# A sixteenth of a PEER layer's experts computed densely beside the gathers of the others

## The reference

```python
q = (ht @ wq).reshape(T, 8, 2, 128)                          # T = 256 tokens, 8 heads
sc = einsum('thpd,hpnd->thpn', q, subkeys)                   # 2 x 128 key scores a head
v1, i1 = top_k(sc[:, :, 0], 16);  v2, i2 = top_k(sc[:, :, 1], 16)
cand = v1[..., :, None] + v2[..., None, :]                   # 256 sums
best, pos = top_k(cand, 16)
experts = i1[pos // 16] * 128 + i2[pos % 16]                 # 16 of 16384 experts, a head
gates = softmax(best)
act = gelu(einsum('tkd,td->tk', u_tab[experts], xb))         # u_tab, v_tab: 16384 x 1024
out = einsum('tk,tkd->td', gates * act, v_tab[experts])
```

## Time and profile before

| | us |
|---|---|
| median of 3 runs | 1186.43 (1185.9 to 1187.0) |
| the profiled execution | 1191.29 |
| its span, first to last instruction | 1189.3 |
| mean granted TensorE clock over the span | 0.988 |

### The profile page before, as it was taken

One profiled execution on the slowest core, in us unless ns is written; L12 is line 12 of the kernel. 1 busy time (PEld: TensorE's weight loads), 2 busy tenths in 40 slices (PEclk: granted clock), 3 DMA queues, 4 the chain that ended last, 5 costly groups with the idle time before them and its releaser, 6 DMA issues.

```text
span 1189.3 us, 14690 instructions
## 1 busy us (share of the span) xinstructions
PE 1055.9 (89%) x4770; PEld 714.6 (60%) x4770; DVE 674.6 (57%) x1469; ACT 531.0 (45%) x1302; POOL 688.3 (58%) x431
## 2 busy tenths in 40 slices
PE   9998998888898877877777778999999999999998
PEld 6874554445454322322232224998999997888886
DVE  2577888877576576784774447323455553521323
ACT  5866434433422322323223235546666435544544
POOL 5734444344444434443344333985797986988885
PEclk9999999999999999899999999999999999999999
DMA  7779999999999999999999997763445554655552
GB/s 254 266 271 422 405 422 420 421 421 422 421 420 421 423 420 420 390 422 422 421 422 422 418 420 296 240 231 111 160 159 160 183 179 153 211 180 195 192 182 102
DMA packets 66530, 372.26 MB, mean 313 GB/s; under 512 B 7672, under 2 KB 8800, under 8 KB 33632
## 3 DMA queue, kind: packets, MB, share of 16 engines
q0 software_dynamic: 37152, 268.45, 54.5%
q1 hardware_dynamic: 26800, 97.02, 24.3%
q10 hardware_dynamic: 2512, 5.94, 1.5%
HBM read 369.80 MB, written 1.06 MB: 312 GB/s over the span
## 4 chain that ended last, share of the span: by engine, by line
PE 53%; DMA 30%; DVE 6%; ACT 5%; issue 4%; POOL 2%; DVEq 0%; ACTq 0%; SPq 0%; POOLq 0%
DMA arena<-in_peer_uv,idx_all 29%; PE ps L1993 12%; PE ps L1680 10%; PE ps L1682 10%; PE ps L1681 10%; PE ps L1704 5%; PE ps L1705 3%; DVE arena L1450 2%; DVE arena L1581 1%; PE ps L2053 1%; ACT prob L807 1%; DMA arena<-in_peer_v,idx_all 1%; POOL w_hl L478 1%; ACT wts L801 1%; POOL arena L494 1%
## 5 line engine op out<-in xcount | busy, mean ns | idle before, releaser
L1993 PE MATMUL ps<-arena,prob 128*128 128x512 f32 x1024 | 476.0, 611 | 117.9 <-ACT prob L807 111.1
L494 POOL DMA_INDIRECT arena<-in_peer_uv,idx_all x254 | 276.0, 1086 | 375.6 <-PE ps L1993 334.2
L478 POOL TENSOR_TENSOR w_hl<-ring,w_hl 128x1024 fp32r<-128x1024 f32 x146 | 368.2, 2534 | 103.5 <-ACT w_hl L585 102.7
L1993 PEld LDWEIGHTS ps<-arena,prob 128*128 128x128 f32 x1024 | 188.3, 193 | 389.8 <-issue 198.9
L1450 DVE CUSTOM_DVE_ANT_0 arena<-arena,xn 128x1024 f32<-128x1024 f32 x256 | 312.2, 1224 | 188.1 <-DMA arena<-in_peer_uv,idx_all 184.8
L794 ACT ACTIVATE gel<-acts 128x2 f32<-128x2 f32 (+1 forms) x131 | 26.7, 204 | 401.2 <-DVE acts L1450 400.8
L585 ACT ACTIVATE w_hl<-ring 128x1024 fp32r<-128x1024 f32 x157 | 165.6, 1060 | 84.1 <-PE ps L1682 80.9
L1680 PE MATMUL ps<-xT,w_hl 128*128 128x256 f32 x568 | 164.1, 289 | 2.4 <-POOL w_hl L478 1.8
L1682 PE MATMUL ps<-xT,w_hl 128*128 128x256 f32 x568 | 161.4, 284 | 0.0
L1681 PE MATMUL ps<-xT,w_hl 128*128 128x256 f32 x568 | 161.3, 284 | 0.0
L1680 PEld LDWEIGHTS ps<-xT,w_hl 128*128 128x128 f32 x568 | 109.6, 193 | 3.8 <-POOL w_hl L478 2.3
(11 more groups left out here) (324 smaller groups left out, 1322.1 us busy)
## 6 DMA issues: line engine op xcount, KB each, us to landing
ring<-in_weights SPq DMA_DIRECT2D x174, 512.0 KB, 3.2
arena<-in_peer_uv,idx_all POOLq DMA_INDIRECT x254
held<-in_weights SPq DMA_DIRECT2D x4, 512.0 KB, 5.7
arena<-in_rg_weights ACTq DMA_DIRECT2D x1, 2048.0 KB, 8.7
bias<-rel_scratch ACTq DMA_DIRECT2D x1, 1024.0 KB, 8.7
arena<-in_subkeys SPq DMA_DIRECT2D x1, 1024.0 KB, 7.1
out_x<-x ACTq DMA_DIRECT2D x4, 256.0 KB, 2.1
arena<-in_band SPq DMA_DIRECT2D x1, 768.0 KB, 7.3
```

What stands on the lines that cost most here:

```text
L478: pool.tensor_tensor(pair[:, 1], raw(n), pair[:, 0].bitcast(F32), ALU.subtract).then_inc(w_lo, 1)
L494: pool.indirect_dma_start(uv_slot(n), None, A["peer_uv"], bass.IndirectOffsetOnAxis(idx_all[:, h, c:c + 1], 0))\
L1993: j = pe.matmul(banks(2 + 2 * t + half), diag[:, n % GRING, :], uv_slot(n)[:, D + half * 512:D + (half + 1) * 512], start=(h == 0 and c % ...
```

## The change

The last 1024 experts (8 values of the first key, "rows") are computed for all 256 tokens from sixteen more weight tiles: eight of the transposed u rows (DU), eight of the v rows (DV). DU and DV are loaded by SyncE behind the query weights, from about slot 82, and are split in high and low at the slots listed (ScalarE `*_HI`, GpSimd `*_LO`).

- Scores: 8 tiles x 12 products into banks 0, 1, 6, 7 behind slots 122, 128, ... 164. One gelu pass of four parts on ScalarE at slot 176, into `x`.
- Gates by threshold: for each head and tile GpSimd adds the two keys' scores for the 1024 experts (128 x 1024); ScalarE exponentiates them; VectorE keeps those at or above the head's 16th best (`least`), multiplies by the softmax's reciprocal sum and adds them to `dense_gates`. That is 16 sums, 16 exponentials and 32 passes of VectorE, at slots 108 to 190.
- Values: gelu times gate (VectorE, slots 190 and 192), 16 transposes (TensorE, 196 and 198), high and low parts into `xT`, and 8 tiles x 12 products behind slots 204, 208, ... 232, added in the banks of the experts.
- Gathers from slot 8 on get `bounds_check=SPARSE - 1` (15359) with `oob_is_err=False`: a row beyond it isn't fetched and the place keeps what lay there. Its gate is multiplied by zero. The first eight gathers fetch all rows. As a left-over row may be used several times, the dot's product goes to a scratch row from slot 12 on, no longer in place; to slot 66 there is one scratch row, and each dot waits for the one before.
- The top-k of heads 3 to 7 starts at slots 64, 80, 96, 112, 128, the gates 16 slots later, with their own buffers (`late_gates`).

```diff
+DENSE_ROWS = 8
+SPARSE_ROWS = NKEYS - DENSE_ROWS
+SPARSE = SPARSE_ROWS * NKEYS
+ODOT_FROM = 12
+BOTH_FROM = 66
+TOPK_FROM = {3: 64, 4: 80, 5: 96, 6: 112, 7: 128}
+DU_HI, DU_LO, DU_AT = ([a + 6 * c for c in range(8)] for a in (108, 119, 122))
+DENSE_EXPS = {0: 108, 1: 120, 2: 132, 3: 144, 4: 154, 5: 164, 6: 174, 7: 184}
+DENSE_GELU = 176
+DENSE_TURN = 196
+DV_AT = [204 + 4 * r for r in range(8)]
+DV_HI = [154 + 6 * r for r in range(4)] + [206 + 4 * r for r in range(4)]
+DV_LO = [a + 11 for a in DV_HI]
@@ sync
+            for n in range(W_DU, W_X2):
+                next_weight(n)
             sp_.wait_ge(v_apart[APART - 1], 16)
@@ gpsimd
                 pool.indirect_dma_start(uv_slot(n), None, A["peer_uv"],
-                                        bass.IndirectOffsetOnAxis(idx_all[:, h, c:c + 1], 0))\
+                                        bass.IndirectOffsetOnAxis(idx_all[:, h, c:c + 1], 0),
+                                        bounds_check=SPARSE - 1, oob_is_err=False)\
+            def dense_key_sums(j):
+                h, t = divmod(j, NT)
...
+                if j >= 2:
+                    pool.wait_ge(dense_kept, j - 1)
+                lanes = scores_of(h).rearrange("p (r n) -> p r n", r=4)
+                pool.tensor_tensor(key_sums(j), bc(lanes[:, 2 * t + 1, :], 1, DENSE_ROWS),
+                                   bc(lanes[:, 2 * t, SPARSE_ROWS:], 2, NKEYS), ALU.add).then_inc(dense_sum, 1)
+            def dense_turn(n):
+                for h, at in DENSE_EXPS.items():
+                    if n in (at + 6, at + 7):
+                        dense_key_sums(2 * h + n - at - 6)
+                if n in DU_LO:
+                    pool.wait_ge(w_lo, W_DU)
+                    split_lo(W_DU + DU_LO.index(n))
+                if n in DV_LO:
+                    split_lo(W_DV + DV_LO.index(n))
@@ scalar
+            def dense_exps(h):
+                for t in range(NT):
+                    j = 2 * h + t
+                    act.wait_ge(dense_sum, j + 1)
+                    act.wait_ge(tk, topk_at(h, t) + 9)
+                    if j >= 2:
+                        act.wait_ge(dense_added, j - 1)
+                    act.activation(key_exps(j), key_sums(j).rearrange("p r n -> p (r n)"), ACT.Exp,
+                                   bias=nbest[:, h, t:t + 1], scale=rinv[:, t:t + 1]).then_inc(dense_exp, 1)
+            def dense_gelus():
+                act.wait_ge(w_used, W_DU + 8)
+                for t in range(NT):
+                    for half in range(2):
+                        act.activation(x[:, t, HALVES[half]], dense_bank(t, half), ACT.Gelu,
+                                       scale=rinv[:, t:t + 1]).then_inc(dense_gelu, 1)
@@ vector
+            def dense_add(j):
...
+                dve.wait_ge(dense_exp, j + 1)
+                dve.scalar_tensor_tensor(out=kept, in0=key_sums(j).rearrange("p r n -> p (r n)"),
+                                         scalar=least[:, h, t:t + 1], in1=kept,
+                                         op0=ALU.is_ge, op1=ALU.mult).then_inc(dense_kept, 1)
...
+                dve.scalar_tensor_tensor(out=dense_gates[:, t, :], in0=kept, scalar=exr[:, h, t:t + 1],
+                                         in1=dense_gates[:, t, :], op0=ALU.mult, op1=ALU.add).then_inc(dense_added, 1)
+                out = u
+                if n >= ODOT_FROM:
+                    out = row_gain[:] if n < BOTH_FROM or n % 2 == 0 else spare_row
...
+                    elif n > ODOT_FROM:
+                        dve.wait_ge(dots_done, n if n <= BOTH_FROM else n - 1)
-                dve.tensor_tensor_reduce(u, u, xn[:, c // TOPK, :], 1.0, 0.0, ALU.mult, ALU.add,
+                dve.tensor_tensor_reduce(out, u, xn[:, c // TOPK, :], 1.0, 0.0, ALU.mult, ALU.add,
-                if 1 < h < PH - 1 and c < TOPK_STAGES:
-                    topk_stage(h + 1, c)
+                for hh, at in TOPK_FROM.items():
+                    if at <= n < at + TOPK_STAGES:
+                        topk_stage(hh, n - at)
@@ tensor
+            def dense_scores(c):
+                w = weight(W_DU + c)
...
+                for t in range(NT):
+                    for half in range(2):
+                        i = matmul3(dense_bank(t, half).rearrange("p (c n) -> p c n", n=P),
+                                    parts(xT, c, slice(t * P, (t + 1) * P)), parts(w, slice(4 * half, 4 * half + 4)),
+                                    c == 0, c == NC_ - 1)
+                i.then_inc(w_used, 1)
+            def dense_values(r):
+                w = weight(W_DV + r)
+                for t in range(NT):
+                    pe.wait_ge(dense_lo, 2 * t + r // 4 + 1)
+                    for half in range(2):
+                        i = matmul3(banks(2 + 2 * t + half).rearrange("p (c n) -> p c n", n=P),
+                                    parts(xT, r, slice(t * P, (t + 1) * P)), parts(w, slice(4 * half, 4 * half + 4)),
+                                    False, False)
+                i.then_inc(w_used, 1)
```

More of the change, by code:

```diff
@@ L169, in build @@
         w_hl = sb("w_hl", [P, SPLIT, 2, NC_, P], F32R)
+        with nc.sbuf_tensor("dense_gates", [P, NT, 1024], F32) as dense_gates:
+            pass
         extra_hl = sb("extra_hl", [P, 2, NC_, P], F32R)
@@ L396, in scores_of, with gates_of, key_sums, key_exps @@
             return sc_all[:, h, :] if h else sc_head0
+        def gates_of(h):
+            return gates[:, h % 2, :] if h < 4 else late_gates[:, h - 4, :]
+        def key_sums(j):
+            return held[:, j % 2, :].rearrange("p (r n) -> p r n", n=NKEYS)
+        def key_exps(j):
+            return held[:, 2 + j % 2, :]
+        def dense_bank(t, half):
+            return banks(DENSE_BANKS[2 * t + half])
         def turn_cols(n, count):
@@ L426, in next_weight @@
             def next_weight(n):
+                at = turn_of(n) % RING
                 sp_.wait_ge(w_lo, n - RING + 1)
-                sp_.dma_start(ring[:, n % RING, :], A["weights"][n]).then_inc(w_ready[n % RING], 16)
+                sp_.dma_start(ring[:, at, :], A["weights"][n]).then_inc(w_ready[at], 16)
             sp_.dma_start(sinks[:], A["sinks"].broadcast_to([P, HEADS])).then_inc(sinks_ld, 16)
@@ L777, in gate_exps, with dense_highs, dense_turn @@
                 for t in tiles:
[L778 to L779 removed]
+                    act.activation(ex[:, h % 2, t, :], best[:, t, :], ACT.Exp, bias=nbest[:, h, t:t + 1],
+                                   scale=rinv[:, t:t + 1], accum_out=exs[:, h, t:t + 1]).then_inc(ex_done, 1)
+            def dense_exps(h):
[13 more added lines that the diff above has]
+                                       scale=rinv[:, t:t + 1]).then_inc(dense_gelu, 1)
+            def dense_highs(t):
+                for half in range(2):
+                    act.wait_ge(dense_turned, 2 * t + half + 1)
+                    act.activation(xT[:, 0, 4 * half:4 * half + 4, t * P:(t + 1) * P],
+                                   dense_bank(t, half).rearrange("p (c n) -> p c n", n=P),
+                                   ACT.Identity).then_inc(dense_hi, 1)
+            def dense_turn(n):
+                for c in range(8):
+                    if n == DU_HI[c]:
+                        split_hi(W_DU + c)
+                    if n == DV_HI[c]:
+                        split_hi(W_DV + c)
+                for h, at in DENSE_EXPS.items():
+                    if n == at:
+                        dense_exps(h)
+                if n == DENSE_GELU:
+                    dense_gelus()
+                for t in range(NT):
+                    if n == DENSE_TURN + 2 * t:
+                        dense_highs(t)
             def x2_square(t):
@@ new lines, in make_gates @@
+                dve.tensor_copy(least[:, h, ts], best[:, ts, TOPK - 1])
+                dve.scalar_tensor_tensor(out=ex[:, h % 2, ts], in0=dec[:, ts, 0, :], scalar=float(SPARSE_ROWS),
+                                         in1=ex[:, h % 2, ts], op0=ALU.is_lt, op1=ALU.mult).then_inc(gt_step, 1)
+                dve.wait_ge(gt_step, 2 * n)
+                if h in (2, 3):
+                    dve.wait_ge(w_done, (h - 1) * SLOTS)
+                dve.tensor_tensor(gates_of(h).rearrange("p (t k) -> p t k", t=NT)[:, ts], ex[:, h % 2, ts],
+                                  bc(exr[:, h, ts], 2, TOPK), ALU.mult).then_inc(gates_done, 1)
@@ L1418, in topk_steps, with dense_turn @@
+            def dense_turn(n):
+                for h, at in DENSE_EXPS.items():
+                    if n in (at + 2, at + 4):
+                        dense_add(2 * h + (n - at - 2) // 2)
+                for t in range(NT):
+                    if n == DENSE_TURN - 6 + 2 * t:
+                        dense_weights(t)
+                    if n == DENSE_TURN + 2 + 2 * t:
+                        dense_lows(t)
             def topk_steps(h, p):
@@ L1441, in late_query @@
                 late, step = divmod(h * SLOTS + 2 * p - LATE_FROM + 2, SLOTS_PER_QUERY)
```

(9 more changed lines are left out.)

116 lines of the change are left out of this document (91 added, 25 removed).

## The result

The changed kernel takes 1222.6 us (median of 4 runs, 1219.9 to 1225.0) against 1186.4 for the kernel before on the same chip (4 runs, 1185.9 to 1187.0): ratio 1.0304, 95% interval 1.0282 to 1.0327, or 36.3 us slower. The forecast was 1183.6 with a range to 1203: wrong in sign, and outside the range. The profiled execution of the kernel before took 1191.3 us, 4.9 over its median, so two profiles laid side by side differ by some 31 us and not by 36.

What follows compares the result with a forecast made beforehand. DMA engines were taken to bound the expert stage, TensorE the stage after. Dropped rows -26.1, early slots +2.4, tile loads +19.9, TensorE's loss +1.0 sum to -2.8 us: 1183.6 against the median 1186.4, range 1174 to 1203.

Steps and rivals of the forecast that it cites:

- the one on ScalarE and GpSimd: Expert stage: GpSimd's 81 us of added sums and low parts fit its idle time; ScalarE's eight stops idle TensorE 3.2 us each.
- Dropped rows: Expert-stage gathers: 1715 rows left out relieve the least relieved DMA engine by 26.1 us, less 2.4 not gained early on.
- Tiles: Expert stage, from slot 82: loading 16 added weight tiles of 512 KB costs the DMA engines 19.9 us.
- DMA net: Expert stage: tile loads of 19.9 us less 26.1 for dropped rows, -6.2 us before the 2.4 not gained early on.
- VectorE "just fits": Slots 110 to 144: VectorE's top-k and dense adds take 39.6 of the DMA's 41 us per 16 slots; loss 0 to 5.
- Stops of ScalarE and TensorE's account: Slots 108 to 232: TensorE's 303 us, eight ScalarE stops included, fit the DMA's 310; 1.0 us lost, bounds 0 to 8.
- The stage behind, unchanged: The stage after the experts is TensorE's and keeps its 453 us.
- The dense steps drain the ring: Rival, slots 108 to 202 and then the values: engines waiting on each other starve the DMA; 1194 to 1205 us; 27%.
- Even relief: Rival, expert-stage gathers: all 16 DMA engines share the dropped rows' time, -33.4 us, so 1176 us; 13%.
- dropped in data only: Rival, expert-stage gathers: dropped rows' packets still take their time or engines stay in step, so 1206 us; 10%.
- packets fall from 37152 by about 1700: Sign of being right: the gathers' queue has about 1700 fewer packets; an unchanged count would point to dropped in data only.
- MB and the weights' queue: Sign of being right: the gathers' queue moves 14 MB less, the queue of weights 8.4 MB more.

Runs made afterwards that it cites:

- the kernel with fills: The kernel before, with 32 GpSimd memory fills (write only, 128x2880) added behind the gathers, nothing dense, all rows fetched: 1190.5 us, ratio 1.0035.
- whole gathers: Kernel without the dense part, 13 whole gathers (1664 rows) dropped and no other row: 1163.0 us against 1188.6 for the kernel before, ratio 0.9770.
- the kernel with all on VectorE: The changed kernel with its 16 sums and 16 low parts made by VectorE, none by GpSimd: 1193.6 us, ratio 1.0076 to the kernel before.
- The kernel that only loads the tiles: The changed kernel without its dense part, rows still dropped, the 16 tiles loaded but unused: 1187.0 us, ratio 0.9996 to the kernel before.

## Why the prediction was wrong

**The step that failed** is the one on ScalarE and GpSimd: "GpSimd's own work grows by 32 x 2.53 = 81 us, and it idled over 330 us". The passes were priced by the idle time of the engine that makes them. They fit there, and GpSimd did have the room; the price was paid on VectorE, 50.5 us of it. The row that should have warned is the prediction's own next one: VectorE at 39.6 of 41 us per 16 slots (its own terms, 16 x 2.38 + 2.7 x 1.25, give 41.5). Of the 32 passes between five and six fall into such a stretch (a head's two sums every 12 slots, a low part every 6), at 50.5 / 32 = 1.6 us each some 8 us of blocking, and 39.6 + 8 does not fit into 41. The measured pace agrees: slots 128 to 144 took 50.1 us. In the kernel before, where VectorE has room, 32 such passes cost 14 us; here taking them off GpSimd won 29 (27 by ratios), although VectorE then made them itself.

The Trainium skill has this behaviour, and I had not weighed it: "SBUF — State Buffer", section "SBUF: two separate sides", says that GpSimd and VectorE share a pair of ports as an exclusive lock, that a VectorE instruction with two SBUF inputs competes for it only against a GpSimd operation that reads SBUF, and that the loser waits for the whole instruction. The traces agree for the dots: 3.67 us over the pass shown, 1.23 on the mean in the kernel with fills.

**The sum by its terms**, with what the runs gave:

- Dropped rows, -26.1 + 2.4 = -23.7: -22.6 alone. Right to 1 us, in part by luck: for whole gathers the same step was 2 to 4 us too high. The edits priced at nothing there (bound check, scratch row, earlier top-k) cost 1.8.
- Tiles, +19.9: +21.1. Right in mechanism, 1.2 low. DMA net +0.3 instead of -3.8.
- VectorE "just fits", 0 to 5: 6.5 with the sums and low parts on it too; as the change has it, VectorE is short by the blocking besides.
- Stops of ScalarE and TensorE's account, +1.0 (bounds to 8): together with GpSimd's passes +29. (The passes took GpSimd 69.6 us, not 81: a sum takes 1.9 us, not 2.53.) TensorE was busy 79% of the 200 us from 360, so its own work was not short of time; it got diagonals late, in waits of up to 8.2 us, and then lost clock: 0.87 granted from 360 to 560 us, a mean between its levels of 1.2 and 2.4 GHz, against 0.98 before.
- The stage behind, unchanged: right, 452 us.

From 1187.0 (tiles loaded) over 1193.6 (dense work, all on VectorE) to 1222.6 (with GpSimd's passes): +6.5 and +29 on the DMA's +0.3 is nearly the whole 36.3, though not all on one chip.

**The rivals.** "The dense steps drain the ring" had the sign, the place (slots 108 to 202) and the symptoms it announced: ten-microsecond windows at 0.75 of DMA, TensorE waiting on diagonals for up to 8.2 us at a time. Its cause was incomplete and its price too low. It counted stops of ScalarE for sums, 2.2 us each at the worst, 1205. The stops are there (31.3 us of waits), but passes for which no engine stops cost 34 to 39 us on top of the kernel with all on VectorE, and VectorE's blocking stood in none of its terms. "Even relief" and "dropped in data only" are refuted as whole cases: 1165.9 with rows dropped is neither -33 nor 0. The prediction's own signal "packets fall from 37152 by about 1700" was wrong: the count is unchanged, and that alone would have spoken for "data only", while the time says otherwise. MB and the weights' queue went as announced.

**Open:** how the 29 us divide between VectorE's blocked passes and ScalarE's waits for late sums, since every run that takes one away takes some of the other (blocking alone is shown to be large enough); how the 6.5 us of the kernel with all on VectorE divide between VectorE's fullness, the exponentials' stops and TensorE's additions; and how much of the 29 us is the clock granted behind the waits rather than the waits. No run holds the clock fixed. The kernel that only loads the tiles was granted 0.94 in the same 200 us and kept the DMA engines at 1.01, so a clock a little lower is not by itself a loss.

## What to carry to other kernels

Before work goes to an engine because that engine is idle, ask which engine it shares a path with and how full that one is: a GpSimd pass that reads the on-chip memory costs a busy VectorE up to about its full length, 1.9 to 2.4 us here (1.6 on the mean of 32), where VectorE would do the same pass in 1.22. An engine's account that fits by 1 or 2 us in 41 is a bound, not a cover; price every new neighbour against it. And where a change trades bytes for bytes, run the two transfers alone first: they came to +0.3 us here, so hiding the compute perfectly would have won nothing measurable.

## What the runs showed of the hardware

- VectorE's pass of two inputs (the dot, 1.22 us) took up to 4.08 us over one GpSimd pass of two inputs (2.36 us; the passes alone in the kernel before), 5.72 us over two in a row, and 1.23 us on the mean in the kernel with fills. Casts of 128x64 went from 0.21 to 1.20 us on the mean of four in the kernel with fills, two of them with a fill beside them (2.79 and 1.62 us). A pass on 128x8 elements with one input, 0.17 us alone, took 3.0 and 3.2 us beside fills of 2.5 us, and 2.2 to 3.1 beside GpSimd passes of two inputs: the price goes by the length of GpSimd's pass and not by that of VectorE's. The finds (284 ns) did not change beside either.
- Beside the about 250 gathers that GpSimd issues in every kernel, dots without a pass beside them stayed at 1.22 us, also the 175 of the changed kernel that ran while a gather was being issued: issuing gathers did not block these dots.
- A row that the bound drops stays as a packet of 4 bytes and 9 ns (315 ns for a row of 8 KB); 1715 of them gave 22.6 us, across two chips. The gather instruction took 1.09 us on the mean before and 1.36 in the expert stage of the changed kernel; with the bound check in place and nothing dropped it took 1.30, at +1.8 us for the kernel.
